# Attention stage of a two-layer backbone: the order of two ScalarE operations in the loop

## What is computed

```
def softmax_attend(q, k, v):
    s = jnp.einsum("bqhd,bkhd->bhqk", q, k).astype(jnp.float32) * (MLA_QK ** -0.5)
    pr = jax.nn.softmax(s, axis=-1).astype(v.dtype)
    return jnp.einsum("bhqk,bkhd->bqhd", pr, v)

# odd_mixer, layer 1: 16 heads, 512 queries in 4 blocks of 128, 768 keys (256 context, 512 latent)
qb = jnp.moveaxis(q_l.reshape(b, nb, Q_BLOCK, MLA_HEADS, MLA_QK), 1, 0)
o = lax.map(lambda qi: softmax_attend(qi, k_all, v_all), qb)
```

## Time and profile before

| | |
|---|---|
| median of 3 runs | 4564.17 us |
| the three runs | 4557.77, 4564.17, 4565.29 us |
| the profiled execution | 4557.77 us, its span 4556.0 us |
| mean granted TensorE clock | 0.829 of full speed |
| attention stage in the span | about 2956.5 to 3141.2 us |
| PE, DVE, ACT, POOL busy in the whole span | 69%, 63%, 24%, 33% |

### The profile page before, as it was taken

How to read it: one execution, slowest core, us unless ns; L and a number is a source line. 1 busy time by engine, 2 the same in 40 slices (tenths; PEclk the granted TensorE clock), 3 DMA queues, 4 the chain that set the end, 5 groups by cost and what they waited for, 6 DMA issues and landing times. The chain is left out here.

```text
span 4556.0 us, 39138 instructions
## 1 busy us (share of the span) xinstructions
PE 3139.6 (69%) x12894; PEld 1434.4 (31%) x12894; DVE 2865.2 (63%) x6905; ACT 1079.5 (24%) x2957; POOL 1494.1 (33%) x1383
## 2 busy tenths in 40 slices
PE   7998989656656656655566665999766665555555
PEld 4645755322222222221122221565432222111111
DVE  1513664677777877885555554564888888555554
ACT  2111232222222222221122211464322222111111
POOL 0000310344444444444344442000344435444443
PEclk9998989877778778777787877999887877777777
DMA  4102651899999999999999998000899999999998
GB/s 165 50 26 72 229 185 31 327 420 420 417 417 415 409 417 417 412 415 422 421 419 421 417 420 350 11 27 31 354 420 419 412 418 404 422 421 422 422 421 349
DMA packets 229515, 1488.34 MB, mean 327 GB/s; under 512 B 25904, under 2 KB 31408, under 8 KB 59072
## 3 DMA queue, kind: packets, MB, share of 16 engines
q0 software_dynamic: 184320, 1342.26, 71.2%
q1 hardware_dynamic: 43616, 139.52, 8.5%
q10 hardware_dynamic: 1376, 4.06, 0.2%
HBM read 1483.61 MB, written 2.13 MB: 326 GB/s over the span
## 5 line engine op out<-in xcount | busy, mean ns | idle before, releaser
L1606 PE MATMUL banks<-arena 128*64 128x512 f32 x5120 | 1616.9, 792 | 1305.6 <-ACT arena L1747 1220.3
L1466 POOL DMA_INDIRECT arena<-experts,arena x1280 | 1421.4, 1110 | 2470.1 <-PE banks L1606 1601.5
L1882 DVE CUSTOM_DVE_ANT_0 arena<-arena 128x1024 f32<-128x1024 f32 x1280 | 1543.5, 1224 | 928.3 <-DMA arena<-experts,arena 901.2
L1606 PEld LDWEIGHTS banks<-arena 128*64 128x64 f32 x5120 | 448.9, 181 | 2382.1 <-ACT arena L1747 1370.5
L1739 ACT ACTIVATE arena<-arena 128x4 f32<-128x4 f32 x320 | 66.1, 207 | 2019.8 <-DVE arena L1882 1984.0
L1747 ACT ACTIVATE arena<-arena 128x64 f32<-128x64 f32 x1280 | 339.3, 335 | 28.5 <-DVE arena L1870 0.4
L1529 PE MATMUL banks<-arena 128*128 128x128 f32 (+2 forms) x1280 | 296.0, 386 | 4.4 <-DMA arena<-wq 3.1
L1529 PEld LDWEIGHTS banks<-arena 128*128 128x128 f32 x1280 | 205.5, 194 | 89.5 <-issue 20.7
L391 PE MATMUL banks<-arena 128*128 128x512 f32 (+1 forms) x640 | 208.6, 486 | 1.9 <-PEq L200 1.9
L732 POOL TENSOR_TENSOR arena<-arena 128x256 f32<-128x256 f32 x48 | 30.4, 634 | 505.1 <-ACT arena L629 375.0
L1480 PE MATMUL banks<-arena 128*128 128x512 f32 x416 | 183.6, 598 | 2.3 <-PEq L826 1.5
(11 more groups left out here) (224 smaller groups left out, 3190.1 us busy)
## 6 DMA issues: line engine op xcount, KB each, us to landing
arena<-l_w_ada SPq DMA_DIRECT2D x48, 1024.0 KB, 5.0
arena<-wq SPq DMA_DIRECT2D x80, 512.0 KB
arena<-experts,arena POOLq DMA_INDIRECT x1280
arena<-l_w_in SPq DMA_DIRECT2D x7, 2048.0 KB, 7.8
arena<-l_w_out SPq DMA_DIRECT2D x4, 1536.0 KB, 12.7
arena<-keys SPq DMA_DIRECT2D x40, 128.0 KB
arena<-l_w_o SPq DMA_DIRECT2D x4, 1024.0 KB, 8.6
arena<-gates SPq DMA_DIRECT2D x6, 512.0 KB, 6.4
```

Source lines behind the costliest of these rows:

```text
L1466: pool.indirect_dma_start(slots[u % NS], None, tbl, bass.IndirectOffsetOnAxis(ap=expert[:, c % RING, k:k + 1], axis=0)).then_inc(land[u % ...
L1606: mm = pe.matmul(core["ps"][QS * j:QS * j + QS, c, :], diag[:, g % 2, k, :], v[:, D + c * 512:D + (c + 1) * 512], start=(g % (NB * PH) == ...
L1882: dve.tensor_tensor_reduce(u, u, rep[i // PH % 2][:, k % NQ, :], 1.0, 0.0, ALU.mult, ALU.add, dots[:, k:k + 1]).then_inc(dot["sem"], up(dot))
```

## The change

On ScalarE, within one pass n of the loop, the exponential of step n is now issued ahead of the copy of step n-2. Both keep their waits. No instruction is added or taken away, and the lists of PE, DVE, POOL and SP stay word for word as they were. Because lines move, the exponential is L1185 and the copy is L1194 in the changed kernel (L1194 and L1187 before).

```diff
@@ def attention_stage, @block.scalar
             for n in range(N + 2):
+                if n < N:
+                    act.wait_ge(mx["sem"], at(mx, n + 1))
+                    if n >= 2:
+                        act.wait_ge(tr["sem"], at(tr, n - 1))
+                    act.activation(pr[n % 2], pair(core, 2 * (n % 2))[:, 0:TOK], ACT.Exp,
+                                   bias=nm[:, n:n + 1], scale=scale,
+                                   accum_out=sm[:, n:n + 1]).then_inc(ex["sem"], up(ex))
                 if n >= 2:
                     u = n - 2
                     m, a, j = u // 4, u // 2 % 2, u % 2
@@
                     act.activation(pt[m % 2][a][:, :, j * P:(j + 1) * P],
                                    pair(core, 4)[:, 0:TOK].rearrange("p (t l) -> p t l", l=P),
                                    ACT.Copy).then_inc(pc["sem"], up(pc))
-                if n < N:
-                    act.wait_ge(mx["sem"], at(mx, n + 1))
-                    if n >= 2:
-                        act.wait_ge(tr["sem"], at(tr, n - 1))
-                    act.activation(pr[n % 2], pair(core, 2 * (n % 2))[:, 0:TOK], ACT.Exp,
-                                   bias=nm[:, n:n + 1], scale=scale,
-                                   accum_out=sm[:, n:n + 1]).then_inc(ex["sem"], up(ex))
```

## The result

| | before | after |
|---|---|---|
| median, first comparison (4 runs each) | 4564.73 us | 4599.61 us |
| ratio, 95% interval | | 1.0080 (1.0062 to 1.0097) |
| profiled execution, its span | 4557.77, 4556.0 us | 4603.26, 4601.4 us |
| PE's first scores of the stage | 2956.56 us | 2960.96 us |
| PE's first matmul behind the stage | 3141.51 us | 3185.72 us |

The changed kernel is slower by 34.9 us, or 0.8%. The forecast was 4608, 43.8 us more than before. The two profiled executions lie 45.5 us apart, but 4.4 us of that had come about before the stage began, in code that both kernels share. So the stage is compared by its own length and not by the span: it is 39.8 us longer. The intervals of all ratios in this document leave out one execution, of the kernel of experiment 3, which took 12828 us where its other nine took 4557.5 to 4565.4.

What follows compares the result with a forecast made beforehand. PE was taken as the bound, busy 49.9 of 50 us in the stage. The loss, 4.2 + 14 x 2.85 = 44.1 us, on the median of 4564.2 gave 4608 us, with a range of 4592 to 4622.

Steps and rivals of the forecast that it cites:

- round: Steady step of the stage: turn, exponential, copy, next turn take 2.88 us against 2.08 before.
- turn to next but one across a weigh: PE around a weigh: from the turn ahead of it to the next but one, 8.29 us against 7.07.
- added up to the first weigh: Start of the stage: first weigh at 2978.95 instead of 2974.74, 4.2 us later.
- exponential with its sum, and the change: On ACT, from exponential's start to copy's start: 1.01 us, made of 0.99 plus a chosen 0.02 for the instruction change.
- low bound of 38 us: Stage's least loss, with 0.02 less per handoff and an overlap of 0.11 between ACT operations; steady round 2.75 us.
- Slack of the copy: In a steady step ACT's copy may come 0.21 us later before PE's next turn is late.
- the ring: Steady steps: turn, exponential, copy and next turn wait on each other in a closed loop, 2.88 us a round.
- marks I named: Signs expected in the changed profile: PE idle 0.8 us before turns, group 14.0 us, stage 228 us, clock 1.00.
- Rival 1: TensorE's clock falls to 1.2 GHz in part of the stage: 4667 us if half the groups ran so; chance 4%.
- Rival 2: PE was waiting for the exponential, so 0.28 us in each of 62 steps come off: 4547 us; chance 3%.
- Rival 3: Another wait of like length behind the turn absorbs the late copy, so the time stays at 4564 us; chance 3%.
- Rival 4: The loop of waits closes only in some steps: about 22 us if two of four are free, 4586 us; chance 6%.

Runs made afterwards that it cites:

- experiment 3: Old order of copy and exponential, with a second pair of PSUM banks for turned probabilities: 4561.43 us, ratio 0.9994 to the kernel before, 11.20 us weigh to weigh.
- second profile of the changed kernel: The changed kernel unaltered, run again beside the kernel before in five rounds: median 4601.83 against 4564.32 us, ratio 1.0084; stage 223.4 us.
- 6: Old order with an additional ScalarE operation of 192 or 576 columns ahead of the copy: 4565.67 and 4581.16 us against 4568.69; 11.32 and 12.11 weigh to weigh.
- 4: Changed order with a third SBUF buffer for the exponentials and one pair of banks: 4594.85 us in one execution, 13.32 us weigh to weigh.
- 5: Old order, exponential first only where n % 4 is 3, or only where 1: 4568.19 and 4581.24 us against 4568.69; 11.20 and 12.19 weigh to weigh.
- experiment 2: Changed order with a second pair of PSUM banks for turned probabilities: 4563.74 us, ratio 0.9998 to the kernel before, 11.39 us weigh to weigh.

## Why the prediction was right, step by step

The mechanism held as forecast, and the size was 44.1 us in the sum against 38.5 in the stage of the second profile of the changed kernel (39.8 in the first).

| step | forecast | measured |
|---|---|---|
| turn to exponential | 0.91 | 0.94 (2975.00 to 2975.94) |
| exponential to copy | 1.01 | 0.89 (2975.94 to 2976.83) |
| copy to next turn | 0.96 | 0.95 (2976.83 to 2977.78) |
| round | 2.88 | 2.78 |
| turn to next but one across a weigh | 8.29 | 8.13 |
| weigh to weigh | 14.05 | 13.69 |
| added up to the first weigh | 4.2 | 3.65 (14.77 from the first turn, 11.12 before) |
| from the last but one weigh to the end | 0 | 0 (9.96 us in both) |
| sum | 44.1 | 3.65 + 14 x 2.49 = 38.5 |

The term that was mis-sized is "exponential with its sum, and the change". I added the end of the READ_ACCUMULATOR and a gap of 0.02. The copy in fact starts 0.10 us before that instruction's recorded end (2976.93), as an ACT operation that starts 0.11 before its predecessor's end was already to be seen in the earlier trace rows. I had taken this overlap as a bound and chosen the gap. The term of 1.01 measured 0.89. The low bound of 38 us in the prediction, which assumed the overlap, came within 0.5 us. The two rounds of a group account for 14 x 2 x 0.10 = 2.8 of the 5.6 us, and the chain across the weigh, which holds the same term once, for 14 x 0.16 = 2.2, of which 0.12 is that term. The range of 30 us was wide enough to hold all this.

Slack of the copy: that there is some is confirmed by 3 (no gain from more banks), its size roughly by 6. The claim that the scores and the peak lie inside the ring: confirmed by 4, in which the peak became the releaser and only 0.37 us came off. That a copy beside a weigh is free: shown by 5. Of the marks I named, the exponential's wait was wrong: it is for the turn in three steps of four and not in two. It waits for the turn ahead of the weigh as well, which costs nothing. The others held in kind and were a little off in size: PE idle for 0.64 us and not 0.8 before a turn, a group of 13.69 and not 14.0, a stage of 223.4 and 224.8 and not 228. The clock below 1 in the stage, which I had named as a sign of being wrong, is there up to the first turns, but in the kernel before as well, and it is no part of the loss in the loop.

Rival 1, the lower clock: the loop ran at 1.00 with PE busy for 41 of 50 us and standing for 0.64 to 1.1 us before three turns of four. What the section of the Trainium skill named in the prediction tells of another kernel (TensorE: Matmul & The Clock Gate, "A second HAM failure mode: psum-queue depth-cycling"), a clock that swings between its two levels, did not happen in this loop. Rival 2, the exponential as the bound: in experiment 2 the exponential starts 0.28 us earlier and the group is no shorter; it falls. Rival 3, absorbed: falls by the result. Rival 4, half of it: three turns of four were late, as the recurrence said.

That the times of the whole (34.9 and 37.5 us) lie a little below the stage's (39.8 and 38.5) is within what runs of one kernel differ by, 8.9 us before and 4.3 us after in the first comparison, and the part behind the stage took the same time in the profiles to within 1.2 us.

## What to carry to other kernels

Where an engine has much idle time, its operations are still not free to change places: ask of each what buffer it hands back, who waits for that buffer, and how much later it may come. Here ACT was 40% idle and the slack of its copy was 0.2 us, since one pair of banks stood behind it. To estimate such a change, follow one step through all engines to the point where the ring closes, and multiply; shares of busy time don't show it. Two repairs are possible, the operation that returns the scarce buffer first or a second buffer. The first costs nothing; the second brought back all but 0.19 us of 2.49 a group here.

## What the runs showed that I had not expected

- After an exponential with a sum, the next ACT operation begins 0.89 us after its start (2975.94 to 2976.83), 0.10 us before the end that the trace gives for the READ_ACCUMULATOR.
- The stage began between 2956.4 and 2963.6 us in eleven profiles of kernels that are the same up to there. For a change of 1% in one stage, the stage's length is the measure, and the span is off by up to 7 us.
- The clock rose earlier in some executions than in others: with 0.67 up to the first turn that turn came 7.05 us after the first scores, with 0.50 it came after 7.88, while from weigh to weigh both profiles of the changed kernel gave 13.69 us.
